# Latent heads: the rotary halves exchanged by VectorE's shuffle in the bank, instead of by a second set of products

## What is computed

```python
def _rope(x, pos):
    half = x.shape[-1] // 2
    ...
    return jnp.concatenate([x1 * cos - x2 * sin, x2 * cos + x1 * sin], axis=-1)

q = (_rmsnorm(q_lat, g_q_lora) @ w_q_up).reshape(b, s, MLA_HEADS, MLA_NOPE + MLA_ROPE)
q_nope, q_pe = q[..., :MLA_NOPE], _rope(q[..., MLA_NOPE:], pos)
kpe = _rope(kpe_raw, pos)
...
logits = (einsum(q_nope, k_nope) + einsum(q_pe, k_pe)) * MLA_SCALE
```

## Time and profile before

| | |
|---|---|
| median of the runs | 1674.59 us |
| the profiled execution's own time | 1674.04 us |
| its span, first to last instruction | 1672.2 us |
| TensorE busy | 1639.2 us, 98% |
| VectorE busy | 1105.0 us, 66% |
| ScalarE busy | 804.4 us, 48% |
| GpSimd busy | 576.6 us, 34% |
| mean granted TensorE clock | 0.998 of full speed |

### The profile page before, as it was taken

One profiled execution on the slowest core, in us unless ns is written; L12 is line 12 of the kernel. 1 busy time (PEld: TensorE's weight loads), 2 busy tenths in 40 slices (PEclk: granted clock), 3 DMA queues, 4 the chain that ended last, 5 costly groups with the idle time before them and its releaser, 6 DMA issues.

```text
span 1672.2 us, 31609 instructions
## 1 busy us (share of the span) xinstructions
PE 1639.2 (98%) x12240; PEld 1589.7 (95%) x12248; DVE 1105.0 (66%) x2047; ACT 804.4 (48%) x1502; POOL 576.6 (34%) x432
## 2 busy tenths in 40 slices
PE   9999999999999999999999999999999999999998
PEld 8989999999998999999999999899989999999998
DVE  5666655555655996587477689533358965874876
ACT  4465555454655654255144445545456541551443
POOL 4453446454553032022013357655550320220122
PEclk9999999999999999999999999999999999999999
DMA  7221223334323133233233322443241332332231
GB/s 193 77 62 53 59 76 98 79 96 108 81 63 80 52 102 114 64 101 104 74 90 88 86 68 69 118 114 89 58 116 52 101 106 71 100 103 76 77 100 58
DMA packets 282744, 145.45 MB, mean 87 GB/s; under 512 B 60334, under 2 KB 273004, under 8 KB 282596
## 3 DMA queue, kind: packets, MB, share of 16 engines
q1 hardware_dynamic: 278136, 136.27, 29.5%
q0 software_dynamic: 3616, 6.92, 1.6%
q10 hardware_dynamic: 844, 0.24, 0.1%
HBM read 130.69 MB, written 15.32 MB: 87 GB/s over the span
## 4 chain that ended last, share of the span: by engine, by line
PE 81%; DVE 11%; ACT 3%; issue 3%; DMA 1%; POOL 1%; SPq 0%; DVEq 0%; ACTq 0%
PE ACC L1269 39%; PE ACC L1682 7%; PE ACC L1684 7%; PE ACC L1683 7%; PE T L1269 3%; PE S L1269 2%; PE ACC L1549 2%; PE S L1524 2%; DVE SCO L2863 2%; DVE TOP L2860 1%; ACT PR L2114 1%; PE S L1684 1%; PE S L1682 1%; PE S L1683 1%; PE T L1537 1%
## 5 line engine op out<-in xcount | busy, mean ns | idle before, releaser
L3502 POOL TENSOR_TENSOR HF<-SG,U 128x576 f32<-128x576 f32 x44 | 65.1, 1478 | 498.4 <-ACT SG L2302 402.3
L1269 PE MATMUL ACC<-XGh,WH 128*128 128x288 f32 (+1 forms) x1008 | 227.6, 307 | 6.7 <-ACT U L2367 2.2
L3347 POOL TENSOR_TENSOR WL<-RAW,WH 128x1024 fp32r<-128x1024 f32 (+3 forms) x84 | 181.4, 2162 | 147.5 <-ACT WH L1989 147.2
L1269 PE MATMUL ACC<-XGh,WL 128*128 128x288 f32 (+1 forms) x1008 | 215.4, 295 | 0.0
L1269 PE MATMUL ACC<-XGl,WH 128*128 128x288 f32 (+1 forms) x1008 | 215.4, 295 | 0.0
L1989 ACT ACTIVATE WH<-RAW 128x1024 fp32r<-128x1024 f32 (+3 forms) x159 | 153.2, 971 | 79.6 <-PE ACC L1269 43.4
L1682 PE MATMUL ACC<-TB,WH 128*128 128x288 f32 x640 | 189.1, 295 | 0.6
L1684 PE MATMUL ACC<-TB,WL 128*128 128x288 f32 x640 | 188.8, 295 | 0.0
L1683 PE MATMUL ACC<-TB,WH 128*128 128x288 f32 x640 | 188.4, 294 | 0.0
L1269 PE MATMUL ACC<-HH,WH 128*128 128x288 f32 x1032 | 179.2, 295 | 0.0
L1269 PEld LDWEIGHTS ACC<-XGh,WH 128*128 128x128 f32 (+1 forms) x1008 | 159.2, 188 | 11.8 <-issue 3.2
(11 more groups left out here) (469 smaller groups left out, 4308.3 us busy)
## 6 DMA issues: line engine op xcount, KB each, us to landing
RAW<-in_w_gate_dram SPq DMA_DIRECT2D x44, 512.0 KB, 3.9
RAW<-in_w_up_dram SPq DMA_DIRECT2D x44, 512.0 KB, 4.6
RAW<-in_w_down_dram SPq DMA_DIRECT2D x32, 512.0 KB, 4.1
RAW<-in_w_in_even_dram SPq DMA_DIRECT2D x29, 512.0 KB, 5.0
RAW<-in_w_in_odd_dram SPq DMA_DIRECT2D x28, 512.0 KB, 4.4
RAW<-in_w_out_even_dram SPq DMA_DIRECT2D x16, 512.0 KB, 4.0
RAW<-in_w_down_dram SPq DMA_DIRECT2D x16, 384.0 KB, 3.5
RAW<-in_w_out_odd_dram SPq DMA_DIRECT2D x8, 512.0 KB, 5.2
```

What stands on the lines that cost most here:

```text
L1269: ins = pe.matmul(out[0:m, 512 * b:512 * b + width], left, right[:, b * width:(b + 1) * width], start=(first and part == 0), stop=(last an ...
L3347: pool.tensor_tensor(WL[slot][:, 0:n], RAW[slot][:, 0:n], WH[slot][:, 0:n].bitcast(F32), ALU.subtract).then_inc(w_lo_pool, 1)
L3502: pool.tensor_tensor(HF[:, q, :], SG[:, q, :], U[:, q, :], ALU.mult).then_inc(h_out, 1)
```

## The change

`ps` is gone: 18 matmuls and its half of the weight unit for each of the four even heads, and its write. The 64 rotary dimensions are laid out so that dimensions that change places lie 16 apart within 32 partitions. After the one product `pe`, VectorE multiplies it by the cosines, shuffles the bank in place (32 partitions at a time), multiplies by the sines in the bank and adds: four linked steps in the place of `pe`'s write. Weights, cosines, sines, and cached keys come in the new order by more DMAs with shorter runs: twelve in place of nine for each `pe` unit, two in place of three for `kp` (both copies now the same), eight in place of two for cosines and sines, five in place of three for the cached latents. `kp`'s columns are put in order as they are split (two instructions on ScalarE and two on VectorE in place of one and one), and CKF gets two copies for a token tile in place of one, the second putting the key back in order.

```diff
 CHUNKS = {
-    "even": [("q", 0, 3), ("k", 0, 2), ("v", 0, 2), ("pe", 0, 3), ("ps", 0, 3), None, None, None],
+    "even": [("q", 0, 3), ("k", 0, 2), ("v", 0, 2), ("pe", 0, 3), None, None, None, None],
...
-    "first even": [("q", 0, 3), ("k", 0, 2), ("pe", 0, 3), ("ps", 0, 3), ("v", 0, 2), None, None, None],
+    "first even": [("q", 0, 3), ("k", 0, 2), ("pe", 0, 3), None, ("v", 0, 2), None, None, None],
...
-            unit("pe", g, cols=2 * QLT * P, end=("ps", g))
+            unit("pe", g, cols=QLT * P, end=("pe", g))
...
-            for n, w in enumerate(("k", "v", "pe", "ps", "q")):
+            for n, w in enumerate(("k", "v", "pe", "q")):
...
+        def halves_apart(rows):
+            return rows.rearrange("p (s q i) -> p q s i", s=2, q=2)
+        def rotary_columns(tile, turned=False):
+            order = "p (m q s i) -> p m q s i" if turned else "p (m s q i) -> p m q s i"
+            return tile[:, :].rearrange(order, q=2, s=2, i=SQUARE // 2)
...
-                    c, r = Q_LORA + KV_LORA, ROPE // 2
-                    return [(0, ROPE, tiles(w_even, 0, DT, c, ROPE)), (ROPE, r, tiles(w_even, 0, DT, c + r, r)),
-                            (ROPE + r, r, tiles(w_even, 0, DT, c, r))]
+                    return [(o, ROPE, tiles(w_even, 0, DT, Q_LORA + KV_LORA, ROPE)) for o in (0, ROPE)]
...
-                        sp.dma_start(dst, pe).then_inc(loaded, 16)
-                        sp.dma_start(dsw[:, :, 0:half], pe[:, :, half:ROPE]).then_inc(loaded, 16)
-                        sp.dma_start(dsw[:, :, half:ROPE], pe[:, :, 0:half]).then_inc(loaded, 16)
+                        for h in range(2):
+                            first = (name[1] + h) * (HD + ROPE) + HD
+                            pe = halves_apart(wq[k * P:(k + 1) * P, first:first + ROPE])
+                            for q in range(2):
+                                dst = raw[:, k * P + h * ROPE + q * SQUARE:k * P + h * ROPE + (q + 1) * SQUARE]
+                                sp.dma_start(dst, pe[:, q]).then_inc(loaded, 16)
...
-            sp.dma_start(COS[:, :], a["cos"]).then_inc(rope_in, 16)
-            sp.dma_start(SIN[:, :], a["sin"]).then_inc(rope_in, 16)
+            for dst, src in ((COS, a["cos"]), (SIN, a["sin"])):
+                for o in range(0, P, SQUARE):
+                    rows = src[o // ROPE * ROPE:(o // ROPE + 1) * ROPE, :].rearrange("(s q i) c -> q s i c", s=2, q=2)
+                    sp.dma_start(dst[o:o + SQUARE, :], rows[o // SQUARE % 2]).then_inc(rope_in, 16)
...
-                prepare(g, "ps", 0, QLT)
...
-                act.wait_ge(acc_free, acc.made("ps", g))
+                act.wait_ge(acc_free, acc.made("pe", g))
...
+            def rotate(out, dst):
+                link(dve.tensor_tensor(two(dst), halves(out), two(COS[:, :]), ALU.mult))
+                link(dve.stream_shuffle(halves(out), halves(out), HALF_SWAP))
+                link(dve.tensor_tensor(halves(out), halves(out), two(SIN[:, :]), ALU.mult))
+                return dve.tensor_tensor(two(dst), halves(out), two(dst), ALU.add)
...
-            lower, upper = slice(0, ROPE), slice(ROPE, P)
-            dve.tensor_tensor(two(YQ[lower, :]), halves(TT)[lower], two(COS[lower, :]), ALU.mult)
-            link(dve.tensor_tensor(two(YK[lower, 0:NT]), halves(TT)[upper], two(SIN[upper, :]), ALU.mult))
-            link(dve.tensor_tensor(YQ[lower, :], YQ[lower, :], YK[lower, 0:NT], ALU.add))
-            dve.tensor_tensor(BO[lower, 0, :], YQ[lower, :], RSTD[lower, :], ALU.mult).then_inc(kp_taken, 1)
-            dve.tensor_tensor(BO[upper, 0, :], YQ[lower, :], RSTD[lower, :], ALU.mult).then_inc(lat_ready, 1)
+            rotate(TT, YQ).then_inc(kp_taken, 1)
+            dve.wait_ge(kp_taken, 1)
+            dve.tensor_tensor(BO[:, 0, :], YQ[:, :], RSTD[:, :], ALU.mult).then_inc(lat_ready, 1)
...
-                    dve.tensor_copy(CKF[0:r, t, :], T[tr.at("lat", t) % 2][0:r, 0:KV_LORA + ROPE]).then_inc(t_free, 1)
+                    out = T[tr.at("lat", t) % 2][0:r, :]
+                    dve.tensor_copy(CKF[0:r, t, 0:KV_LORA], out[:, 0:KV_LORA])
+                    dve.tensor_copy(halves_apart(CKF[0:r, t, KV_LORA:KV_LORA + ROPE]),
+                                    out[:, KV_LORA:KV_LORA + ROPE].rearrange("p (q s i) -> p q s i", q=2, s=2)).then_inc(t_free, 1)
...
-                        ins = dve.tensor_tensor(two(rotated(g)), halves(out), two(COS[:, :]), ALU.mult)
-                    elif what == "ps":
-                        link(dve.tensor_tensor(halves(out), halves(out), two(SIN[:, :]), ALU.mult))
-                        dve.wait_ge(acc_free, acc.made("pe", g))
-                        ins = dve.tensor_tensor(two(rotated(g)), halves(out), two(rotated(g)), ALU.add)
+                        ins = rotate(out, rotated(g))
...
-                write_projection(g, "ps")
```

More of the change, by code:

```diff
@@ L72 @@
 SQUARE, QUADRANTS = 32, P // 32
+HALF_SWAP = [(i + SQUARE // 2) % SQUARE for i in range(SQUARE)]
 BIG = -1.0e30
@@ L341, in plan_attention @@
                 r, what, k0, k1, total = c
-                if k0 == 0 and what not in ("v", "ps") or (k0 == 0 and what == "v" and kind_of(r) != "mla"):
+                if k0 == 0 and what != "v" or (k0 == 0 and what == "v" and kind_of(r) != "mla"):
                     if kind_of(r) != "mla":
@@ L349, in plan_attention @@
                     else:
-                        unit("pe", r, cols=2 * QLT * P, end=("ps", r), in_slot=True)
+                        unit("pe", r, cols=QLT * P, end=("pe", r), in_slot=True)
                 if k1 == total:
@@ L354, in plan_attention @@
                         finished.append((what, r))
-                    elif what in ("q", "v", "ps"):
-                        finished.append(({"v": "kv", "ps": "pe"}.get(what, what), r))
+                    elif what in ("q", "v", "pe"):
+                        finished.append(({"v": "kv"}.get(what, what), r))
             if h < 16 and g is not None and s == k_job_slot(g) == 5:
@@ L554, in build @@
     unit_dmas = {n: 1 for n in units.names}
-    unit_dmas[("kp",)] = 3
+    unit_dmas[("kp",)] = 2
     for n in units.names:
         if n[0] == "pe":
-            unit_dmas[n] = 3 * QLT
+            unit_dmas[n] = 4 * QLT
         if n[0] == "kv":
@@ L992, in _ @@
             load_unit("kp")
-            sp.dma_start(COS[:, :], a["cos"]).then_inc(rope_in, 16)
-            sp.dma_start(SIN[:, :], a["sin"]).then_inc(rope_in, 16)
+            for dst, src in ((COS, a["cos"]), (SIN, a["sin"])):
+                for o in range(0, P, SQUARE):
+                    rows = src[o // ROPE * ROPE:(o // ROPE + 1) * ROPE, :].rearrange("(s q i) c -> q s i c", s=2, q=2)
+                    sp.dma_start(dst[o:o + SQUARE, :], rows[o // SQUARE % 2]).then_inc(rope_in, 16)
             sp.dma_start(CCK[:, 0:KV_LORA], a["cache_mla_ckv"][0, 0]).then_inc(cc_in, 16)
-            for o in (0, ROPE):
-                sp.dma_start(CCK[:, KV_LORA + o:KV_LORA + o + ROPE], a["cache_mla_kpe"][0, 0]).then_inc(cc_in, 16)
+            for o in range(0, P, SQUARE):
+                sp.dma_start(CCK[:, KV_LORA + o:KV_LORA + o + SQUARE],
+                             halves_apart(a["cache_mla_kpe"][0, 0])[:, o // SQUARE % 2]).then_inc(cc_in, 16)
             sp.wait_ge(acc_free, acc.made("vrow"))
@@ L1444, in prepare @@
                     latent_product(("q", g), ("q", g), 0, P, k0, k1, QLT, QGh, QGl, HALF)
-                elif what in ("pe", "ps"):
-                    latent_product((what, g), ("pe", g), 0 if what == "pe" else QLT * P, P, k0, k1, QLT, QGh, QGl, HALF)
+                elif what == "pe":
+                    latent_product(("pe", g), ("pe", g), 0, P, k0, k1, QLT, QGh, QGl, HALF)
                 else:
@@ L1988, in unit_hi @@
                     act.wait_ge(*room)
+                if name == ("kp",):
+                    old, new = rotary_columns(RAW[slot]), rotary_columns(WH[slot], turned=True)
+                    act.activation(new[:, :, 0], old[:, :, 0], ACT.Copy)
+                    act.activation(new[:, :, 1], old[:, :, 1], ACT.Copy).then_inc(w_hi, 1)
+                    return
                 act.activation(WH[slot][:, 0:n], RAW[slot][:, 0:n], ACT.Copy).then_inc(w_hi, 1)
@@ L2531, in unit_lo @@
                 slot = slot_of[name]
+                if name == ("kp",):
+                    old, new, high = rotary_columns(RAW[slot]), rotary_columns(WL[slot], turned=True), rotary_columns(WH[slot], turned=True)
+                    dve.tensor_tensor(new[:, :, 0], old[:, :, 0], high[:, :, 0].bitcast(F32), ALU.subtract)
+                    dve.tensor_tensor(new[:, :, 1], old[:, :, 1], high[:, :, 1].bitcast(F32), ALU.subtract).then_inc(w_lo, 1)
+                    return
                 dve.tensor_tensor(WL[slot][:, 0:n], RAW[slot][:, 0:n], WH[slot][:, 0:n].bitcast(F32),
```

15 lines of the change are left out of this document (5 added, 10 removed).

## The result

Six executions of each kernel on one chip: 1681.52 us median (1680.54 to 1689.12) against 1674.32 (1673.68 to 1676.32), ratio 1.0054 with a 95% interval of 1.0032 to 1.0075. The change costs 7.2 us by the medians where I had forecast 3.8. The ratio goes by the means, and by them it costs 9.0, since two of the six executions took 1687.68 and 1689.12. The direction holds, and the median lies inside the range, but the cost is about twice the forecast.

A forecast was written before the change was run, and what follows sets the result against it. VectorE's four-step block, then ScalarE, set the pace where products go, despite TensorE's 98% busy time. Heads 3 and 5 2.5, head 1 1.06, copies 0.16, `kp` 0.1 sum to +3.8: 1674.59 + 3.8 = 1678.4 us, range 1674.5 to 1683.0.

The forecast's parts named there:

- Heads 3 and 5: VectorE's block delays row maxima and scaled probabilities, the removed product gains nothing, the next bank comes late: +1.25 us each.
- Head 1: The block makes tile 3's row maxima 2.0 us late and the next head's first scores late: +1.06 us.
- the opening's block: In the opening the four steps put q's write 0.06 us early, VectorE alone setting it: taken as zero.
- the links: VectorE steps cost 0.80 us linked, 0.68 unlinked; by the skill's page, block 0.36 us shorter, four places 1.4 less.
- the shuffle's bounds: Shuffle between 0.22 and 1.54 us, moving each of four places by -0.55 or +0.77: 1676.2 to 1681.5 us.
- two late copies: Two more tiles of split CKF copies on the path in head 0, at 81.6 us: +0.16 us.
- `kp`'s 0.1: Splitting the key weights `kp` in two instructions per engine, close to the product waiting for them: +0.1 us.
- The gaps cool TensorE: Rival, 0.12: TensorE's clock falls in new idle stretches of the opening and heads 1, 3, 5: up to +8, around 1683.
- The price of the exchange: In VectorE's block the shuffle costs about 0.77 us, like a 32 x 32 transpose, plus 0.08 for loading its list.
- The cancelled lag: Rival, 0.15: later ScalarE and VectorE steps close up, so heads 3 and 5 cost nothing, head 1 +1: 1675.8 us.
- The products come out: Rival, 0.07: each of the four removed products saves 2.67 us of the time, -10.7: 1663.9 us.
- Loads are late: Rival, 0.06: shorter runs or SP's extra issues in the opening make a latent's weights late: +2 and more, about 1680.

The follow-up runs named there:

- e15: Changed kernel with unread matmuls filling TensorE's waits in the opening and head 1, not in heads 3 and 5: 1679.34 us, ratio 1.002 to the kernel before.
- e6: Kernel before with each of the four second products cut to one one-column matmul, VectorE's steps unchanged: 1672.81 us, ratio 0.9984.
- e5: The changed kernel run again, unaltered: 1682.9 us, ratio 1.0041 to the kernel before.
- e1: Changed kernel with 18 unread matmuls in each of TensorE's waits in the opening and heads 1, 3 and 5: 1680.0 us, ratio 1.0027 to the kernel before.
- e4: Changed kernel with TensorE's warm-up at 18 matmuls in place of 14: 1682.66 us.
- the first profile: Profile of the changed kernel's slowest execution among the six of the result: 1689.12 us.
- e14: Changed kernel with only the opening reordered: VectorE copies and clears upper key rows before the value product, takes first latents before the query: 1679.46 us, ratio 1.0018.
- e3: Changed kernel with the exchange of halves (the shuffle) left out at all five rotations: 1678.84 us, ratio 1.0025 to the kernel before.
- e9: Changed kernel with the opening reordered and the rotation's four steps apart, exchange, sine step and sum in PSUM: 1673.49 us, ratio 0.9997 to the kernel before.
- e11: e10 plus eight unread matmuls, starting their own group, in TensorE's wait at the end of the first layer's attention: 1672.09 us, ratio 0.9985.
- e12: Kernel before plus only the eight unread matmuls of e11 in the same wait: 1674.56 us, ratio 0.9998.
- e13: e11 with the eight matmuls not starting or stopping a group (start and stop False): 1672.34 us, ratio 0.9986 to the kernel before.
- e10: e9 plus six unread matmuls in one TensorE wait of each of heads 1, 3 and 5: 1674.1 us, ratio 0.9994 to the kernel before.

## Why the prediction was half right

The lags of VectorE's block, which made up the sum, came as reckoned, but for 0.5 us in the opening. The step that failed is that the sum had no term for TensorE's clock: its fall behind the new waits stood as a rival at 0.12, and it cost 2.5 to 4.1 us in the profiles, up to as much as all lags.

*The lags.* e15 shows them with no fall that costs anything. Heads 3 and 5: 2.77 - 1.57 = 1.20 and 4.15 - 2.96 = 1.19, forecast 1.25 each; the block of 3.08 us and all that follows it stood as reckoned. Head 1: 1.70 - 0.79 = 0.91, forecast 1.06. The products saved nothing there, as I had said. In sum 4.27 at head 16, forecast 3.8, and the time 1679.34 against a median of 1675.4. The forecast's sum took nothing for the opening's block, so what the prediction works out from the Trainium skill for the links would have made it 1.1 us less and not 1.4, and the shuffle's bounds, over three places and not four, would have made 1676.8 to 1680.7.

*The opening was mis-sized.* I had 0.16 for two late copies and 0.1 for `kp`; it is 0.79. Up to the first scores nothing came late, `kp`'s 0.1 neither: the query's write, forecast 0.06 early, came at 75.62 in e15 against 75.88, and TensorE's third turn at 76.90 against 77.09. The loss comes at 82.5, in a step that I had not looked at, the low part of the odd head's rotated query. Timelines of VectorE and GpSimd, the kernel before, then e15:

```profile
82.51 0.75 DVE L2727 TENSOR_TENSOR QPO<-BO,QPO 64x576 fp32r<-64x576 f32 x1
...
82.63 1.52 POOL L3347 TENSOR_TENSOR WL<-RAW,WH 128x384 fp32r<-128x384 f32 x1 [2.28 <-ACT WH L1989]
```
```profile
82.45 1.61 DVE L2761 TENSOR_TENSOR QPO<-BO,QPO 64x576 fp32r<-64x576 f32 x1
...
82.44 1.01 POOL L3380 TENSOR_TENSOR WL<-RAW,WH 128x384 fp32r<-128x384 f32 x1 [2.29 <-ACT WH L2015]
```

Both steps read two tensors in SBUF. Before, VectorE began 0.12 us earlier and GpSimd waited (1.52 in place of 1.01); now GpSimd begins 0.01 us earlier and VectorE waits (1.61 in place of 0.75). GpSimd came 0.19 earlier than before, like the turns, and VectorE only 0.06: the two tiles of split copies take 0.13 more (0.16 forecast), and the loser changed; behind it the next query's write comes 0.79 late (84.19 against 83.40). Every profile with split copies shows 1.61 or 1.62 us here, the kernel before and e6, which keep the single copies, 0.75 and 0.76.

*The sum left out TensorE's clock.* This is the step that failed: "The gaps cool TensorE" was a rival at 0.12 and no term. The waits were forecast to within 0.3 us (about 3, 2.5, twice 2; measured 2.9, 2.5 and 2.7, 1.7 and 1.8), so the condition was known. Behind CKF the fall cost 3.59 - 0.87 = 2.72 us (e5 less e1; less e4, where the same wait brought no fall, 2.66), behind head 1 it cost 5.86 - 4.49 = 1.37. Together 4.1, as much as all lags. The size varies: behind head 1 it was 2.35 in the first profile, 2.47 in e4 and 2.60 in e14, and e4, with nothing behind CKF, lost 2.5 in all. The rival's own time, around 1683, is what e5 measured, 1682.9. "Against: some of these gaps are broken by scores and turns" was no reason: head 1's two waits, with 0.6 us of turns between them, were enough. Right was "where no other engine is the later one": the falls in heads 3 and 5 cost nothing. Once I had written that the waits arise, the case in which they bring no fall needed the evidence, not the other; but falls in heads 3, 5 and in e4's opening did also fail to come, so a share of the executions, not all, was the thing to forecast. How large that share is stays open; there are only a few profiles.

*The price of the exchange* was right (0.76 and 0.01, taken as 0.77 and 0.08), and e3 shows that it comes out whole. The links cost 0.80 - 0.68 as before: 163.63 - 162.83 with one, 165.91 - 165.23 without, where the page of the Trainium skill that the prediction cites, VectorE: DVE Perf Modes, section "The DRAIN you can't avoid", says that a semaphore costs nothing extra; the measurement decides. *The cancelled lag* (0.15) did not occur: e1 and e15 show 1.2 in heads 3 and 5. *The products come out* (0.07) did not occur either, and e6 shows that the price I gave it, -10.7, was not to be had in this order of the work. *Loads are late* (0.06) did not occur: in e15 TensorE's third turn of the opening comes 0.19 us earlier than in the kernel before.

## What to carry to other kernels

Work that is taken from the busiest engine is not time gained until something follows that could have started earlier: before removing a product, find what else is late at that point, and count the idle stretch as a cost of its own, since the clock may fall behind it and the work behind runs at half pace. When a step of several instructions replaces one, put the next tile's short step between them (ratio 1.0018 to 0.9997, e14 to e9), and look at which bank they hold meanwhile. A fall of the clock is worth nothing where a later engine sets the next start, and up to its full length where TensorE does.

## What the runs showed that I had not expected

- The same wait can have a fall behind it in one execution and none in another: 2.46 and 2.47 us in head 3 (0.62 in one profile, 1.00 in the other), 1.17 us at the layer's end (1.00 and 0.66). The Trainium skill, TensorE: Matmul & The Clock Gate, Part 1, says that the chip's watch on TensorE runs freely and not from the kernel's start; the rows fit that, without proving it. It makes part of a kernel's spread.
- VectorE's steps with both inputs in SBUF take 1.61 to 2.24 us in place of 0.75 where GpSimd subtracts at the same time; in the opening the later of the two pays. The same steps with one operand in PSUM stay at 0.77 (e9). A buffer that frees a bank early cost 2.9 us in a head, more with a fall of the clock, and a start that moved by a tenth of a microsecond cost 0.8.
- A matmul that starts a group in free columns of a bank disturbs the sum that is pending in its other columns (e11 and e12 against e13).
- Unread matmuls in a wait can pay: in the changed kernel they took the ratio from 1.0041 or more (e4, e5) to 1.0020 (e15). In e10 six of them, ahead of head 1's last turn, brought 2.7 us in the profile, the twelve in heads 3 and 5 nothing, and the median did not fall.
